# Turning features into the array in fewer, longer groups, in a float32 transformer kernel that TensorE fills

## The reference

```
h  = x + mixer1(rmsnorm(x))                 # stick-breaking attention + HGRN2, ends with w_out
h  = h + square(relu(rmsnorm(h) @ w_ff1)) @ w_ff2
h  = rmsnorm(h)
for layer in 0, 1:
    h = h + mix(rmsnorm(h))                 # layer 0: gated linear attention, layer 1: differential attention
    h = h + swiglu(rmsnorm(h))              # ends with ffn_w_out
    h = h + sigmoid(rmsnorm(h) @ w_gate) * (p @ w_proj)
```

## Time and profile before

| what | value |
|---|---|
| median of 3 runs | 1028.85 us |
| the profiled execution: its own time | 1028.49 us |
| its span on the core | 1026.7 us |
| TensorE busy (PE) | 1020.5 us, 99% |
| weight loads (PEld, beside PE) | 934.8 us, 91% |
| VectorE (DVE) | 862.0 us, 84% |
| ScalarE (ACT) | 658.4 us, 64% |
| GpSimdE (POOL) | 70.9 us, 7% |
| DMA | 185.46 MB, mean 181 GB/s |

### The profile page before, as it was taken

One profiled execution on the slowest core, in us unless ns is written; L12 is line 12 of the kernel. 1 busy time (PEld: TensorE's weight loads), 2 busy tenths in 40 slices (PEclk: granted clock), 3 DMA queues, 4 the chain that ended last, 5 costly groups with the idle time before them and its releaser, 6 DMA issues.

```text
span 1026.7 us, 17540 instructions
## 1 busy us (share of the span) xinstructions
PE 1020.5 (99%) x7069; PEld 934.8 (91%) x7069; DVE 862.0 (84%) x1074; ACT 658.4 (64%) x800; POOL 70.9 (7%) x53
## 2 busy tenths in 40 slices
PE   9999999999999999999999999999999999999998
PEld 8998999889999999888999999989888899999997
DVE  6888887689999978965898998777989699888874
ACT  6777545567666666765755656476777667555654
POOL 0000001200000030002004600010000200000010
PEclk9999999999999999999999999999999999999999
DMA  9746354655666646455565656555424456566641
GB/s 303 237 173 202 125 187 142 194 186 187 196 202 205 203 146 206 140 187 174 164 204 169 222 168 225 171 193 171 164 83 160 138 201 210 169 200 204 198 173 42
DMA packets 126657, 185.46 MB, mean 181 GB/s; under 512 B 3184, under 2 KB 97904, under 8 KB 126576
## 3 DMA queue, kind: packets, MB, share of 16 engines
q1 hardware_dynamic: 125984, 183.27, 54.4%
q0 software_dynamic: 160, 0.52, 0.2%
q10 hardware_dynamic: 432, 0.53, 0.2%
HBM read 183.26 MB, written 1.05 MB: 180 GB/s over the span
## 4 chain that ended last, share of the span: by engine, by line
PE 99%; DMA 0%; ACT 0%; DVE 0%; SPq 0%; issue 0%
PE PS L511 97%; PE PS L519 2%; DMA RAW<-in_w_in_dram 0%; ACT AR L1949 0%; DVE AR L2894 0%; DVE H L2896 0%; ACT WH L1431 0%; SPq L3189 0%
## 5 line engine op out<-in xcount | busy, mean ns | idle before, releaser
L511 PE MATMUL PS<-Z,WH 128*128 128x256 f32 (+1 forms) x2608 | 484.4, 288 | 1.5 <-ACT WH L1431 1.1
L511 PEld LDWEIGHTS PS<-Z,WH 128*128 128x128 f32 x2608 | 407.9, 192 | 7.2 <-ACT WH L1431 1.3
L2135 DVE TENSOR_TENSOR WL<-RAW,WH 128x2048 fp32r<-128x2048 f32 (+4 forms) x172 | 349.6, 2039 | 49.8 <-ACT WH L1431 48.9
L511 PE MATMUL PS<-Z,WL 128*128 128x256 f32 x1352 | 370.9, 284 | 0.0
L511 PE MATMUL PS<-WH,Z 128*128 128x512 f32 (+1 forms) x1226 | 356.0, 366 | 0.0
L1431 ACT ACTIVATE WH<-RAW 128x2048 fp32r<-128x2048 f32 (+4 forms) x183 | 314.0, 1719 | 62.3 <-PE PS L511 51.5
L511 PEld LDWEIGHTS PS<-Z,WL 128*128 128x128 f32 x1352 | 255.5, 191 | 2.7
L511 PEld LDWEIGHTS PS<-WH,Z 128*128 128x128 f32 x1226 | 220.7, 189 | 35.8 <-issue 1.8
L511 PE MATMUL PS<-WL,Z 128*128 128x512 f32 (+1 forms) x613 | 222.2, 363 | 0.0
L511 PEld LDWEIGHTS PS<-WL,Z 128*128 128x128 f32 x613 | 116.1, 189 | 15.1
L511 PE MATMUL PS<-Z 128*128 128x512 f32 (+1 forms) x388 | 93.2, 388 | 0.0
(11 more groups left out here) (219 smaller groups left out, 771.1 us busy)
## 6 DMA issues: line engine op xcount, KB each, us to landing
RAW<-in_ffn_w_in_dram SPq DMA_DIRECT2D x44, 1024.0 KB, 5.2
RAW<-in_w_ff_dram SPq DMA_DIRECT2D x32, 1024.0 KB, 5.4
RAW<-in_ffn_w_out_dram SPq DMA_DIRECT2D x22, 1024.0 KB, 5.1
RAW<-in_w_in_dram SPq DMA_DIRECT2D x18, 1024.0 KB, 5.6
RAW<-in_gla_w_in_dram SPq DMA_DIRECT2D x12, 1024.0 KB, 5.4
RAW<-in_diff_w_in_dram SPq DMA_DIRECT2D x12, 1024.0 KB, 5.2
RAW<-in_ple_w_gate_dram SPq DMA_DIRECT2D x8, 1024.0 KB, 5.2
RAW<-in_w_out_dram SPq DMA_DIRECT2D x4, 1024.0 KB, 5.1
```

Of the source, the lines that this page charges most:

```text
L511: return e.matmul(o, l, r, start=start, stop=stop, skip_group_check=skip)
L2135: e.tensor_tensor(low, raw, high.bitcast(F32), ALU.subtract).then_inc(s["w_lo"], 1)
```

## The change

The lists of the eight feature blocks are regrouped. In `g2`, `nm0`, `nf0` and `nf1` the groups were {0,1} {2,3} {4} {5} {6} {7}, where {0,1} stood in `down_last` and the others ahead of k = 0, 1, 2, 3 and 4; now they are {0,1,2,3} in `down_last`, {4,5} ahead of k = 1 and {6,7} ahead of k = 3. In `pn0` and `pn1` the six groups become {0,1} in `down_last`, {2,3} ahead of k = 0, {4,5} ahead of k = 2, and {6,7} behind the first k of the second half of the tokens. In differential attention `turn_q(2)` moves behind `pair(0, 0, 1)` to stand with `turn_k(2)`, `turn_a(1)` moves behind `pair(1, 0, 0)` to stand with `scores(5)`, and `values(4)` moves behind three quarters of `back(0, 1)` to stand with `turn_o(1)`. ScalarE's copy `a_turned(1)` moves behind two other steps, and VectorE's `turning(3, 0)` ahead of `difference(3)`. No instruction is added or removed on a compute engine.

```diff
-    AHEAD = {"nm1": ((), (), (), (6,), (7,)), **{f"pn{i}": ((2, 3), (4,), (5,), (6,), ()) for i in range(2)}}
+    AHEAD = {"nm1": ((), (), (), (6,), (7,)), **{f"pn{i}": ((2, 3), (), (4, 5), ()) for i in range(2)}}
+    AT_LAST = {f"pn{i}": (0, 1) for i in range(2)}

     def ahead(name, k):
-        steps = AHEAD.get(name, ((2, 3), (4,), (5,), (6,), (7,)))
+        steps = AHEAD.get(name, ((), (4, 5), (), (6, 7)))
...
-        for j in AHEAD.get(norm, ((2, 3),))[0]:
+        for j in AHEAD.get(norm, ((),))[0]:
             h_step(norm, j)
...
                 if n == 1 and tb == 1:
                     free()
-                    h_step(norm, 0)
-                    h_step(norm, 1)
+                    for j in AT_LAST.get(norm, (0, 1, 2, 3)):
+                        h_step(norm, j)
...
         toks_long(c, 0, (3, 4), ops, (0,), f"pn{layer}", free)
-        h_step(f"pn{layer}", 7)
-        toks_long(c, 0, (3, 4), ops, (1,), None, free)
+        toks_long(c, 0, (3, 4), ops, (1,), None, free, range(1))
+        for k in (6, 7):
+            h_step(f"pn{layer}", k)
+        toks_long(c, 0, (3, 4), ops, (1,), None, None, range(1, 4))
...
     pair(0, 0, 0)
+    pair(0, 0, 1)
     e.wait_ge(s["df_qk"], 4)
     turn_q(2)
-    pair(0, 0, 1)
     turn_k(2)
...
     pair(0, 1, 1)
+    pair(1, 0, 0)
     turn_a(1)
-    pair(1, 0, 0)
     scores(5)
...
     back(0, 0)
+    back(0, 1, ((0, 0), (0, 1), (1, 0)))
     values(4)
-    back(0, 1, ((0, 0), (0, 1), (1, 0)))
...
-    a_turned(1)
     evac_pair(0, 1)
     hi(d0 + 12)
+    a_turned(1)
...
+    turning(3, 0)
     difference(3)
-    turning(3, 0)
```

## The result

| | before | after |
|---|---|---|
| median of 17 runs each | 1028.85 us | 1030.84 us |
| lowest to highest | 1028.15 to 1030.21 | 1029.99 to 1031.55 |
| span of the profiled execution | 1026.7 us | 1029.6 us |

The ratio is 1.0019, 95% interval 1.0012 to 1.0025. The forecast was 1030.0 us in 1028.3 to 1031.0.

The account below looks back on a forecast made before the run. TensorE, busy 99% of the span, was taken as the bound. Waits of 1.28 us minus 0.1 saved by joins gave +1.2 us, so 1030.0 us from 1028.85, in the range 1028.3 to 1031.0.

Parts of the forecast that it names:

- A boundary is nearly free: Transpose groups everywhere: 0.005 us per vanished boundary, between -0.02 and +0.03; 19 joins save 0.1 us.
- Rival 2: Behind each transpose group: the slow matmul (0.09 us) is lost time, so 19 joins remove 1.7 us; chance 0.09.
- The fourth add makes block 4 wait: g2, nf0, nf1, nm0: TensorE waits for VectorE's add ahead of k = 1, 0.31 us each, 0.35 in nm0.
- Rival 1: Four stages: the add is early enough, blocks 4 and 5 don't wait, only the saving is left, 1028.5 us; chance 0.15.
- `pn0` and `pn1` cost nothing: pn0, pn1: later blocks 4 to 7 cost nothing, covered by nine or more matmuls (2.0 us) before `turned` needs them.
- The attention costs nothing: Differential attention: its three moves are covered by spare time, priced at 0, bounds -0.1 to +0.3 us.
- Rivals 3 and 4: Four stages: late low parts hold k = 2, 1031.2 us, chance 0.08; clock falls in long groups, 1033.5 us, chance 0.02.
- the dearer waits for the add: Four stages: upper bound of the wait for the add, 0.4 us each if the release is dearer, 1.6 in all.
- rival 3: Four stages: VectorE's low parts of block 2 come late and hold k = 2, time 1031.2 us; chance 0.08.

Follow-up runs that it names:

- e7_apart: Kernel before with the second transposes of blocks 4 to 7 in four stages set apart, 16 more boundaries: 1029.19 us against 1029.08 for the kernel before.
- e4_attention: Kernel before with only the change's moves in differential attention, on all three engines: 1028.31 us, ratio 0.9988 to 1.0005.
- e8_late_and_first: Kernel after with blocks 4 and 5 ahead of k = 2 in four stages and ScalarE's weight rounding first in ple: 1028.53 us against 1029.08 before.
- e1_four_late: Kernel after with blocks 4 and 5 of g2, nm0, nf0, nf1 ahead of k = 2 instead of k = 1: 1029.54 us, ratio 0.9997 to 1.0015.
- e5_four_early: Kernel after with blocks 4 and 5 of the four stages ahead of k = 0, 6 and 7 ahead of k = 2: 1035.04 us.
- e2_pn_back: Kernel after with pn0 and pn1 grouped as before, six groups each: 1029.85 us, ratio 1.0002 to 1.0020.
- e6_weight_first: Kernel after with ScalarE's rounding of ple's third weight chunk ahead of its copies of blocks 6 and 7: 1029.73 us, ratio 0.9998 to 1.0016.
- e10_add_last: e5_four_early with block 4 waiting for its bank first and the add last: 1033.52 us, ratio 1.0031 to 1.0065.
- e9_half_early: Kernel after with blocks 4 and 5 of four stages in the middle of k = 0, 6 and 7 ahead of k = 2: 1031.56 us.

## Why the prediction was right, point by point, and what it missed

*A boundary is nearly free.* Right in the main. `e7_apart` added 16 and moved nothing. The joins in the attention gave 0.22 us for three, 0.07 each and not 0.005: there the bound of 0.03 was too low. The prediction had seen a part of it, that matmuls just behind a group run slower than steady, but priced it at nearly nothing. Behind `turn_q(2)` at its old place seven 512-column matmuls took 1.62 us (750.63 to 752.26 in the kernel before); with the group moved away, seven in `e4_attention` took 1.59 (750.62 to 752.21). In `nf0` the wait of 0.31 cost 0.24, so three joins gave 0.07. All 19 together gave 0.3 us in `e8_late_and_first`, by its trace. Rival 2, that the slow matmul behind each group is lost time, 1.7 us in all, fell.

*The fourth add makes block 4 wait, 0.31 us in three stages and 0.35 in `nm0`, 1.28 in all.* Right in place, cause and size: k = 1 started within 0.01 us of the forecast in both timelines, and taking the wait away in `e1_four_late` gave 1.30 us by the medians and 1.2 by the stages. Rival 1 is out. `e5_four_early` shows the dose: more of it costs more, though there a dearer release comes on top.

*`pn0` and `pn1` cost nothing.* Wrong, and worth some 0.95 us by the traces, 0.99 by the medians of `e2_pn_back` and the kernel after. (The 0.78 us in the expectations is twice the 0.39, without the late matmul behind it.) The sentence that failed is "the cover is the nine or more 512-column matmuls (2.0 us) before `turned` asks for them". That is the cover of TensorE's own need of blocks 6 and 7. The prediction didn't ask what is queued behind their copies on ScalarE and VectorE: the factors, a table load of 1.3 us, 1.9 us of rounding and 2.3 us of rest for a weight chunk, with 0.6 us to spare before the change. `e6_weight_first` shows that it was that queue, as nothing of TensorE's order is changed in it.

*The attention costs nothing.* Right; all three covers held, and `e4_attention` shows no wait.

*Rivals 3 and 4.* TensorE was never held at k = 2. TensorE's granted clock stayed at 1.00, the 2.4 GHz level, over the new group of eight transposes, by the windows view of the kernel after (columns as in the earlier trace rows):

```profile
200.97:201.84 0.87, 0.87 (x10) 0.86 (x8) 0.67 (x1) 0.73 (x4) 0.87 (x1) 1.00 0.09 20
```

The Trainium skill, "TensorE: Matmul & The Clock Gate", Part 4 (PE-mode transpose), has it that transposes don't count as TensorE activity as matmuls do. Groups of this length, between matmuls, gave no sign that it matters here: eight transposes and the matmul behind them took 1.11 us in `g2` of the kernel after (200.97 to 202.08), as in the prediction's group of eight.

*The sum.* Forecast +1.2 us, measured +1.99. It is the sum of a term that was right (1.28), one that was put at nothing (0.95), and joins that gave a little more than was taken (0.3 instead of 0.1): 1.9. That the time fell into the range is in part luck. A loss of nearly 1 us was not in it, and what made room for it was the upper bounds of other terms, the dearer waits for the add and rival 3, none of which came. Of the chances, "within 0.2%" got 0.86, and the ratio of 1.0019 lies at its edge.

## What to carry to other kernels

Where the bounding engine hardly waits, a reordering has little to win (0.3 us for 19 joins here) and can lose whatever it uncovers: before moving a step earlier, subtract from its new due time the end of what it needs; before moving one later, walk down the queue of every engine that works on its result, as the next user may be another transfer or weight chunk altogether. The spacing of starts says what a kind of instruction costs; a slow instruction behind a change of kind need not be lost time. If a wait must stay, put it behind the waits that are fulfilled already, and look whether it sits on the load or stands as an instruction of its own.

## What the runs showed that was not expected

Fulfilled waits behind a late one were dear where they were instructions of their own on TensorE: 0.21 us for two of them (`e5_four_early` against `e10_add_last`). Where the late wait sat on the load itself, the load followed the add's end by 0.05 us, after 0.3 us of standstill too (`e9_half_early`).

The profiled execution of the kernel after was 1.0 us behind in the first 10 us, which the change doesn't touch. The timeline there, before and then after, shows four 256-column matmuls in a row from 7.07 to 7.81, with a wait among them, and then eight by 8.85, 0.12 to 0.13 each; after, six from 6.02 on take until 7.47, over 0.2 each, and the next four until 8.32, 0.2 each:

```profile
7.07 0.63 PE L511 MATMUL PS<-Z,WL 128*128 128x256 f32 x4
7.81 1.20 PE L511 MATMUL PS<-Z,WH 128*128 128x256 f32 x8
8.85 0.64 PE L511 MATMUL PS<-Z,WL 128*128 128x256 f32 x4
```

```profile
6.02 1.65 PE L511 MATMUL PS<-Z,WH 128*128 128x256 f32 x6 [0.64 <-ACT WH L1434]
7.47 1.05 PE L511 MATMUL PS<-Z,WL 128*128 128x256 f32 x4
8.32 1.49 PE L511 MATMUL PS<-Z,WH 128*128 128x256 f32 x6
```

The windows view reads a granted clock of 1.00 over the first 10 us of both, so the trace doesn't say that it was the clock, and the cause stays open. It comes and goes between executions of kernels that are alike there: at about 10 us `e8_late_and_first` was 0.97 behind the kernel before and `e1_four_late` 0.63 ahead. A difference of this size in the start is enough to explain why runs of one kernel spread by over 1 us, and single executions can't tell 0.1% apart here, while stages of two traces can.
